# Channel mixing of a two-layer decoder trunk by Strassen's scheme, with weight sums on GpSimd

## What is computed

```python
for l in range(DEPTH):                                   # 2 layers
    u = _rmsnorm(h, norm_mix_pre[l])
    mix, v_first = _mixer(u, ...)
    h = h + _rmsnorm(mix, norm_mix_post[l])
    u = _rmsnorm(h, norm_ffn_pre[l])
    f = jnp.square(jax.nn.relu(u @ w_up[l])) @ w_down[l] # 1024 -> 4096 -> 1024
    h = h + _rmsnorm(f, norm_ffn_post[l])
```

## Time and profile before

| | us |
|---|---|
| median of 3 runs (4385.25 to 4389.9) | 4388.46 |
| the profiled execution | 4390.43 |
| its span, first to last instruction | 4388.7 |

### The profile page before, as it was taken

One profiled execution on the slowest core, in us unless ns is written; L12 is line 12 of the kernel. 1 busy time (PEld: TensorE's weight loads), 2 busy tenths in 40 slices (PEclk: granted clock), 3 DMA queues, 4 the chain that ended last, 5 costly groups with the idle time before them and its releaser, 6 DMA issues.

```text
span 4388.7 us, 66844 instructions
## 1 busy us (share of the span) xinstructions
PE 3986.1 (91%) x28112; PEld 2674.6 (61%) x28112; DVE 1744.9 (40%) x3846; ACT 771.4 (18%) x1536; POOL 213.3 (5%) x188
## 2 busy tenths in 40 slices
PE   7999677999979999999899986869999899999996
PEld 4566455885656666666555654558855566666663
DVE  2599766665140000000247988566641400000002
ACT  1211452331010000000112124523310100000000
POOL 0041000000000000000001310000000000000000
PEclk9999798998989999999999988879979999999997
DMA  2001000001111111111310110100011111111112
GB/s 109 25 29 39 35 18 2 3 3 47 54 58 38 36 36 38 39 33 38 116 34 24 39 29 13 35 2 3 3 62 38 60 37 38 38 34 38 38 38 83
DMA packets 43313, 162.71 MB, mean 37 GB/s; under 512 B 5056, under 2 KB 5072, under 8 KB 42720
## 3 DMA queue, kind: packets, MB, share of 16 engines
q1 hardware_dynamic: 27648, 100.68, 7.6%
q0 software_dynamic: 15456, 58.85, 3.6%
HBM read 135.07 MB, written 23.49 MB: 36 GB/s over the span
## 4 chain that ended last, share of the span: by engine, by line
PE 82%; DVE 13%; issue 3%; ACT 2%; DMA 0%; POOL 0%; DVEq 0%; ACTq 0%; POOLq 0%
PE ps L544 46%; PE ps L576 16%; PE ps L618 7%; PE ps L767 1%; PE ps L779 1%; DVE arena L1207 1%; PE ps L821 1%; PE ps L792 1%; DVE arena L1328 1%; PE ps L588 1%; PE ps L554 1%; DVE arena L1179 1%; DVE arena L1330 1%; DVE arena L1186 1%; DVE arena L1327 1%
## 5 line engine op out<-in xcount | busy, mean ns | idle before, releaser
L544 PE MATMUL ps<-arena,ring 128*128 128x348 f32 x6912 | 2035.4, 458 | 28.8 <-DVE arena L1158 18.9
L544 PEld LDWEIGHTS ps<-arena,ring 128*128 128x128 f32 x6912 | 1321.4, 191 | 743.8 <-issue 42.8
L576 PE MATMUL ps<-arena,ring 128*128 128x348 f32 x2304 | 697.7, 462 | 23.3 <-DVE arena L1158 18.9
L576 PEld LDWEIGHTS ps<-arena,ring 128*128 128x128 f32 x2304 | 437.1, 192 | 282.7 <-issue 54.6
L618 PE MATMUL ps<-arena 64*64 64x64 f32 (+1 forms) x13600 | 513.2, 226 | 97.7 <-DVE arena L1282 43.2
L618 PEld LDWEIGHTS ps<-arena 64*64 64x64 f32 x13600 | 467.9, 135 | 141.9 <-DVE arena L1328 48.8
L1167 DVE TENSOR_TENSOR aux<-arena 128x1044 f32<-128x1044 f32 x32 | 39.9, 1246 | 1068.2 <-ACT arena L938 1068.2
L938 ACT ACTIVATE arena<-ps 128x1044 f32 x96 | 99.9, 1040 | 1971.6 <-PE ps L544 1971.6
L1207 DVE TENSOR_SCALAR_CACHE_REDUCE arena<-arena,little 128x384 uint8<-128x384 f32 (+6 forms) x448 | 416.9, 991 | 3.1
L1561 DVE TENSOR_TENSOR arena<-arena x64 | 79.8, 1246 | 812.2 <-ACT arena L938 812.2
L989 ACT ACTIVATE arena<-ps 128x128 f32<-128x128 f32 x340 | 93.3, 277 | 192.5 <-PE ps L618 192.5
(11 more groups left out here) (202 smaller groups left out, 2612.3 us busy)
## 6 DMA issues: line engine op xcount, KB each, us to landing
ring<-units SPq DMA_DIRECT2D x192, 512.0 KB, 3.6
h_scratch<-arena POOLq DMA_DIRECT2D x24, 522.0 KB, 3.1
arena<-h_scratch POOLq DMA_DIRECT2D x24, 522.0 KB, 7.5
arena<-h_in POOLq DMA_DIRECT2D x16, 522.0 KB, 9.9
out<-arena POOLq DMA_DIRECT2D x8, 522.0 KB, 3.1
arena<-att_scratch POOLq DMA_DIRECT2D x2, 2080.0 KB, 9.0
att_scratch<-arena POOLq DMA_DIRECT2D x16, 256.0 KB, 2.9
aux<-rope POOLq DMA_DIRECT2D x2, 1044.0 KB, 12.4
```

Source lines behind the costliest of these rows:

```text
L544: ins = mm(ps[:, b + s, 0:SW], ring[:, (u % RING) * D + k * P:(u % RING) * D + (k + 1) * P], rhs(g * KT + k)[:, slice_(s)], start=(g == 0 ...
L576: ins = mm(ps[:, b + s, 0:SW], ring[:, r * D + k * P:r * D + (k + 1) * P], tile(U0, k)[:, slice_(s)], start=(k == 0), stop=(k == KT - 1))
```

## The change

Channel mixing is cut into quarters of the 4096 hidden channels. For quarter n, an up step (q = 2n) multiplies a 1024 by 1024 square of `w_up` with the input, and a down step (q = 2n + 1) a square of `w_down` with the 1024 new hidden channels, adding to the output. A step is 4 pairs of units, j = 0 to 3. Units a and b of a pair are cut into halves along their inputs, which gives four blocks of 128 outputs by 512 inputs; the right operand is cut into upper and lower 4 tiles, and left and right SPLIT = 522 tokens. A pair's 2 by 2 product of blocks is formed by Strassen's scheme (Winograd's form) with seven products in place of eight. Each product accumulates over 4 blocks in two slices of HALF = 261 tokens in two banks; four such accumulators take turns.

- The sums of right operands (four a step, 128 by 4 x 522) are VectorE's (`operand_sums`), once for the input and once a quarter for the hidden channels.
- The four sums of weights a pair (128 by 512 each) are GpSimd's (`weight_sums`), in two buffers.
- ScalarE copies out the first product of a pair alone (`first_of`). VectorE adds up all seven (`quarters`), rectifies and squares in one operation (`scalar_tensor_tensor`, max then mult), and in the last step squares the outputs for the norm.
- The SyncE queue is unrolled, follows the new order of units, and refills both slots of a pair when all its seven products are done.
- GpSimd loads `h` again (into `U0`) between the weight sums of q = 6 and q = 7, when q = 6 has ended on TensorE. The load of `small` for layer 1 moves behind the first `h_ready`.
- All of channel mixing is unrolled on TensorE. The output tiles are at `OUT0`; `rstd` and the squares move to `Z0` and behind.

The core of the diff:

```diff
+SPLIT, HALF = W // 2, W // 4
+SQUARES = FFN // D
+PRODUCTS = 7
+PAIRS = 2 * SQUARES * KT // 2
...
+        acc_at = lambda n: ps[:, 2 * (n % 4):2 * (n % 4) + 2, 0:HALF]
...
+            for at in range(DEPTH * UNITS):
+                k = at % RING
+                if at >= RING:
+                    l, pos = divmod(at - RING, UNITS)
+                    if pos < NZ + KT:
+                        sp.wait_ge(S["unit_done"], l * (NZ + KT) + pos + 1)
+                    else:
+                        sp.wait_ge(S["products"], PRODUCTS * (l * PAIRS + (pos - NZ - KT) // 2 + 1))
+                sp.dma_start(ring[:, k * D:(k + 1) * D], units[source(at)]).then_inc(landed[k], 16)
...
+                def weight_sums(l, q, j):
+                    p = l * PAIRS + q * KT // 2 + j
+                    pos, a, b = pair_slots(q, j)
...
+                    for k in (a, b):
+                        pool.wait_ge(landed[k], 16 * ((l * UNITS + pos) // RING + 1))
+                    if p >= 2:
+                        pool.wait_ge(S["products"], PRODUCTS * (p - 1))
+                    for i, x, y, op in ((1, quarter(b, 0), quarter(b, 1), ALU.add),
+                                        (2, w_sum(p, 1), quarter(a, 0), ALU.subtract),
+                                        (3, quarter(a, 0), quarter(b, 0), ALU.subtract),
+                                        (4, quarter(a, 1), w_sum(p, 2), ALU.subtract)):
+                        nc.gpsimd.tensor_tensor(w_sum(p, i), x, y, op).then_inc(S["weights_ready"], 1)
+                        pool.wait_ge(S["weights_ready"], w.next("weights_ready"))
...
-                pool.wait_ge(S["h_stored"], w.next("h_stored", 16 * KT))
-
-                pool.wait_ge(S["unit_done"], (l + 1) * UNITS - (FFN // D - 1))
-                for k in range(KT):
-                    dma(res_at(k), h_dram[k], "h_loaded")
+                for q in range(2 * SQUARES):
+                    for j in range(KT // 2):
+                        weight_sums(l, q, j)
+                    if q == 2 * SQUARES - 2:
+                        pool.wait_ge(S["h_stored"], w.next("h_stored", 16 * KT))
+                        pool.wait_ge(S["products"], PRODUCTS * (l * PAIRS + (2 * SQUARES - 1) * KT // 2))
+                        for k in range(KT):
+                            dma(res_at(k), h_dram[k], "h_loaded")
...
+            def seven(l, q, j):
...
+                fresh = j == 0 and (q == 0 or q % 2 == 1)
+                def product(i, lhs, rhs, sums=0, weights=0, ready=None):
+                    n = PRODUCTS * p + i
+                    if n >= 4:
+                        pe.wait_ge(S["acc_free"], n - 3)
+                    if fresh and sums:
+                        pe.wait_ge(S["sums_ready"], have + sums)
+                    if weights:
+                        pe.wait_ge(S["weights_ready"], 4 * p + weights)
+                    for k in range(KT // 2):
+                        if ready:
+                            pe.wait_ge(S["u_ready"], ready + k)
+                        for s in range(2):
+                            ins = mm(acc_at(n)[:, s], lhs[:, k * P:(k + 1) * P], rhs(k)[:, s * HALF:(s + 1) * HALF],
+                                     start=(k == 0), stop=(k == KT // 2 - 1))
+                    ins.then_inc(S["products"], 1)
...
+                product(0, quarter(a, 0), lambda k: upper(k, 0), sums=1 if q else 0, ready=first)
+                product(1, quarter(a, 1), lambda k: lower(k, 0), sums=3 if q else 0, ready=first and first + 4)
+                product(2, w_sum(p, 2), t_(2), sums=4, weights=2)
+                product(3, w_sum(p, 3), lambda k: upper(k, 1), sums=5, weights=3)
+                product(4, w_sum(p, 1), t_(1), weights=1)
+                product(5, quarter(b, 1), t_(4), sums=6)
+                product(6, w_sum(p, 4), lambda k: lower(k, 1), weights=4)
...
-                project(MT_FFN, lambda k: tile(U0, k), base + NZ + KT, ready=("u_ready", 2 * KT * l + KT, range(1, KT + 1)))
-                pe.wait_ge(S["hid_ready"], w.next("hid_ready"))
-                project(KT, lambda k: tile(HID0, k), base + NZ + KT + MT_FFN, group=FFN // D)
+                for q in range(2 * SQUARES):
+                    for j in range(KT // 2):
+                        seven(l, q, j)
...
+                for p in range(l * PAIRS, (l + 1) * PAIRS):
+                    act.wait_ge(S["products"], PRODUCTS * p + 1)
+                    if p:
+                        act.wait_ge(S["acc_free"], PRODUCTS * (p - 1) + 3)
+                    go(halves(first_of), acc_at(PRODUCTS * p), ACT.Copy).then_inc(S["first_out"], 1)
...
+                fresh = q % 2 == 0 or q == 1
+                if not fresh:
+                    dve.wait_ge(S["first_out"], p + 1)
+                    add(c[0][0], c[0][0], first)
+                dve.wait_ge(S["products"], n + 2)
+                dve.wait_ge(S["first_out"], p + 1)
+                add(c[0][0], first if fresh else c[0][0], m2, 2)
+                if q % 2 == 0:
+                    rectified(c[0][0])
+                dve.wait_ge(S["products"], n + 3)
+                add(c[0][1] if fresh else u, first, m6, 1)
+                if not fresh:
+                    add(c[0][1], c[0][1], u)
+                dve.wait_ge(S["products"], n + 4)
+                add(u, c[0][1] if fresh else u, m7, 1)
+                if not fresh:
+                    add(c[1][1], c[1][1], u)
+                    add(c[1][0], c[1][0], u)
+                dve.wait_ge(S["products"], n + 5)
+                add(c[1][1], u if fresh else c[1][1], m5)
+                add(c[0][1], c[0][1], m5, 1)
+                dve.wait_ge(S["products"], n + 6)
+                add(c[1][0], u if fresh else c[1][0], m4, 1)
...
+                    if k == KT // 2 - 1:
+                        dve.wait_ge(S["u_ready"], w.value("u_ready"))
+                        dve.sem_inc(S["sums_ready"], 1)
+                        operand_sums(U0, TU0, 1, 0, 4)
...
+                        quarters(l, q, j)
+                        if q % 2 == 0 and j == 1:
...
+                            operand_sums(HID0, TH0, 1, 0, 4)
+                        if q % 2 == 0 and j >= 2:
+                            for i in (2, 3, 4):
+                                operand_sums(HID0, TH0, i, 2 * j - 4, 2 * j - 2, last=j == 3)
```

More of the change, by code:

```diff
@@ L421, in _, with source @@
         def _(sp):
[L422 to L429, removed]
+            def source(at):
+                l, pos = divmod(at, UNITS)
+                if pos < NZ + KT:
+                    return at
+                q, i = divmod(pos - NZ - KT, 2 * KT)
+                first = l * UNITS + NZ + KT
+                return first + KT * q + i if i < KT else first + MT_FFN + SQUARES * (i - KT) + q
+            for at in range(DEPTH * UNITS):
+                k = at % RING
+                if at >= RING:
+                    l, pos = divmod(at - RING, UNITS)
+                    if pos < NZ + KT:
+                        sp.wait_ge(S["unit_done"], l * (NZ + KT) + pos + 1)
+                    else:
+                        sp.wait_ge(S["products"], PRODUCTS * (l * PAIRS + (pos - NZ - KT) // 2 + 1))
+                sp.dma_start(ring[:, k * D:(k + 1) * D], units[source(at)]).then_inc(landed[k], 16)
         @block.gpsimd
@@ L601, in out_of @@
                 pe.wait_ge(tri(name), tri_out(l, name))
+            def seven(l, q, j):
+                p = l * PAIRS + q * KT // 2 + j
+                pos, a, b = pair_slots(q, j)
+                raw, t = (U0, TU0) if q % 2 == 0 else (HID0, TH0)
+                have = sums_of(l, 0 if q % 2 == 0 else 1 + q // 2)
+                quarter = lambda k, right: ring[:, k * D + right * 4 * P:k * D + (right + 1) * 4 * P]
+                upper, lower = (lambda k, side: side_of(raw, k, side)), (lambda k, side: side_of(raw, 4 + k, side))
+                t_ = lambda i: (lambda k: t_at(t, i, k, k + 1)[:, 0])
+                fresh = j == 0 and (q == 0 or q % 2 == 1)
[14 more added lines that the diff above has]
+                    ins.then_inc(S["products"], 1)
+                for k in (a, b):
+                    pe.wait_ge(landed[k], 16 * ((l * UNITS + pos) // RING + 1))
+                first = 2 * KT * l + KT + 1 if fresh and q == 0 else None
+                product(0, quarter(a, 0), lambda k: upper(k, 0), sums=1 if q else 0, ready=first)
[5 more added lines that the diff above has]
+                product(6, w_sum(p, 4), lambda k: lower(k, 1), weights=4)
             def pe_chunk(w, odd):
@@ new lines, in quarters, with add, rectified, squared @@
+            def quarters(l, q, j):
+                p = l * PAIRS + q * KT // 2 + j
+                base = HID0 if q % 2 == 0 else OUT0
+                c = [[halves(side_of(base, 2 * j + k, side)) for side in range(2)] for k in range(2)]
+                n = PRODUCTS * p
+                m2, m6, m7, m5, m4, m3 = (acc_at(n + i) for i in range(1, PRODUCTS))
+                first, u = halves(first_of), halves(u_sum)
```

(24 more changed lines are left out.)

89 lines of the change are left out of this document (67 added, 22 removed).

## The result

| | before | after | ratio |
|---|---|---|---|
| median of the first comparison, us | 4389.18 (4 runs) | 4176.20 (4170.34 to 4186.01) | 0.9515, interval 0.9492 to 0.9537 |
| median of a second, 9 runs and 5 | 4391.79 | 4177.89 (4173.12 to 4181.97) | 0.9517, interval 0.9504 to 0.9530 |
| the profiled execution | 4390.43, span 4388.7 | 4186.01, span 4184.1 | |

The change takes 213 us off. 4168 was forecast, from 222.1 us less, with 4150 to 4235 as its range.

The account below looks back on a forecast made before the run. TensorE's streamed matmul columns were taken to bound channel mixing. Its terms, 1577.0 + 12.7 + 1.0 - 0.6 = 1590.1 us in place of 1812.2, took 222.1 off 4390.43, giving 4168; range 4150 to 4235, 8 in 10.

Parts of the forecast that it names:

- What binds: Channel mixing, 1812.2 us for two layers, is bound by TensorE's streamed matmul columns alone; VectorE works 10% there.
- Part 1: Seven products a pair in channel mixing: 7168 records of 261 columns at 220.0 ns, 1577.0 us for both layers.
- the price of a matmul: TensorE's 348-column record costs 292.5 ns, 2.5 fixed; the remaining 1.8 us of half a layer belong to hardware loops.
- Part 2: TensorE's waits for accumulators and sums are met and cost nothing visible, with 7 to 10.6 us of slack.
- rival (a): TensorE's waits between products each expose a 107 ns weight load: +48 us, 4216; 12%.
- Part 3: VectorE's rectification and recombination, at worst 13.1 of 24.64 us a pair, stay hidden, cost 0; both 3.0 us holes go.
- Rival (b): VectorE, held by GpSimd, is late at some products: 1.2 us a pair, +77 us, 4245; 6%.
- Part 4: GpSimd's weight sums in channel mixing take 1.2 us each, 4.9 us a pair, and are ready in time: cost 0.
- The hold between GpSimd and VectorE: Each GpSimd weight sum can hold VectorE for its own length, at most 4.9 us a pair: still hidden, cost zero.
- part 6: GpSimd's reload before the last quarter delays the next weight sums: 0.5 us a layer, 6.6 if sums await the transfers.
- Part 5: At each layer's start the first pair waits for tiles and operand sums: 6.4 us lost, 12.7 for both layers.
- rival (c): Shorter matmuls leave the weight load uncovered: 325 ns a record, 4904 us, slower than before from 251 ns; 4%.

Follow-up runs that it names:

- e1_eight: Changed kernel with the second product of every pair streamed twice, so eight products a pair: 4395.25 us.
- e6_waits: Changed kernel with three more already met waits on the accumulator in each TensorE product from the fifth on: 4170.00 us.
- e5_260: Changed kernel with each matmul streaming 260 columns in place of 261: 4174.30 us.
- e3_pool2: Changed kernel with every GpSimd weight sum computed twice: 4205.24 us.
- e9_order: e8_start with VectorE taking out the first two products between the second and third operand sums: 4165.93 us, ratio 0.9487 to the kernel before.
- e7_reload: Changed kernel with the weight sums of the last quarter's first pair put ahead of the reload of h: 4174.77 us.
- e4_dve2: Changed kernel with each VectorE addition done twice, first into a spare place: 4187.27 us.
- e8_start: e7_reload with each layer's first pair reordered, products without operand sums earlier, VectorE's sums after all tiles: 4175.93 us, ratio 0.9509 to the kernel before.

## Why the prediction held, and where it was off

- **What binds** (first part): right. e1_eight shows it most plainly. VectorE's 10% holds for the up halves alone; in the down halves it is 16.2 of 451 us.
- **Part 1, 220.0 ns a record**: 220.7 measured. 0.7 ns x 7168 = 4.9 us, the largest share of the 7.8 us by which the stage fell less than forecast (214.3 against 222.1). The mechanism was right and the fixed part mis-sized: I took 2.5 ns from 348 columns, and it is 3.2. Neither waits nor the odd count explain the rest (e6_waits, e5_260), and its cause stays open.
- **The 1.8 us put down to hardware loops** (the price of a matmul): this reading was wrong, though nothing in the sum hangs on it. The down half of layer 0 before, from its start and then from 1709.6 us on:

```profile
1705.20:1709.60 4.40, 4.33 (x9) 2.67 (x10) 0.00 (x0) 0.00 (x0) 0.00 (x0) 0.61 0.01 3
1709.60:2156.50 446.90, 446.90 (x1528) 290.42 (x1526) 16.20 (x13) 7.28 (x7) 4.70 (x9) 1.00 0.15 48
```

  In the loops 446.90/1528 = 292.5 ns, as in the unrolled part. What is over lies in the first 4.4 us, at a granted clock of 0.61, behind the 3.0 us hole. The change takes that away with the hole.
- **Part 2, waits**: right at zero, and rival (a) with its 48 us is refuted by e6_waits.
- **Part 3, VectorE hidden**: right. An addition of 522 columns with an operand in PSUM took 699 ns (0.70 forecast), the stage had VectorE at 322.3 of 802.8 us, 40%. Doubling the additions moved the stage by 4.6 us. Rival (b) asked for 77 us; none of it is seen.
- **Part 4, weight sums**: 1.27 us each at their median, 1.2 forecast, and hidden, by e3_pool2 with room for twice as much in the midst of the stage, but not at its start. That the first sums end 0.2 us ahead of the tiles was not in my working; the zero there was right by luck.
- **The hold between GpSimd and VectorE**: it exists as forecast. The prediction has it hidden, and so it is in the midst of the stage; at the reload it lies on the path (part 6). One line of VectorE, its operands told apart (ns min/median/max, first to last start):

```profile
L1336 DVE TENSOR_TENSOR arena<-arena,ps x200: 698/699/701, 1281.9 to 4138.4; 128x522 f32<-128x522 f32 x100
L1336 DVE TENSOR_TENSOR arena<-arena,aux x96: 702/703/1687, 1565.8 to 4129.3; 128x522 f32<-128x522 f32 x96
```

200 additions with one operand in PSUM were never held, and among 96 with both in SBUF some stood up to a microsecond. GpSimd's sums have the same mark, 1261 ns at least and up to 2157. This agrees with the Trainium skill (SBUF — State Buffer, Who interferes with whom): the shared port pair is an exclusive lock, a VectorE instruction with two SBUF inputs contends with a GpSimd instruction that reads SBUF, and one with at most one SBUF input, outside the 2-port modes, does not.

- **Part 5, the start**: third product at +15.15 us after the first tile began, +14.8 forecast: 0.35 a layer. The clock brought no surprise here: it was at 1.00 before the second product began, in both layers. Of the 6.6 us that the first pair loses against seven products of 3.53 (6.4 forecast), e9_order gets 3.8 back.
- **Part 6, the reload**: 1.4 us a layer, 0.5 forecast, 1.9 in all. The step that failed is "the first two sums, 2.4 us": they took 1.29 and 2.17, since the second met VectorE's operand sum (L1320). That is the hold between the two engines, which the prediction had priced at zero. e7_reload removes the hole. The high bound of 6.6, sums behind the transfers, is refuted: the first sum starts as the eighth issue ends.
- **The slower side**, rival (c): 220.7 ns a record, against 251 where it would begin. A load per record is covered as before. (Its 4904 leaves out the 13.1 us of the other terms; with them it is 4917.)
- **The level of the total**: forecast 4168 for the profiled execution, 4186 measured there, 4176 and 4178 as medians. Of the profiled one's 18 us, 8 are the stage's and 10 token mixing's, whose matmuls the change leaves as they were. There, layer 0 began channel mixing 7.0 us later than before, 0.5 of it from before 1042 us. The windows of before and of after over the same gate matmuls, in this order:

```profile
1042.00:1058.00 16.00, 15.21 (x33) 6.78 (x34) 8.08 (x7) 2.08 (x2) 0.00 (x0) 0.78 0.00 0
```

```profile
1042.00:1058.00 16.00, 14.70 (x23) 6.08 (x24) 8.16 (x7) 1.04 (x1) 0.00 (x0) 0.58 0.00 0
```

At a granted clock of 0.78 TensorE did 33 records in those 16 us, at 0.58 it did 23. The clock fell at 1044.6 us in place of 1050.9 and stayed at 0.50 for 54.6 us in place of 40.9. In another execution of the changed kernel channel mixing began at 1245.1, 4.5 us earlier than before, and over the traces of the changed kernel and its variants it began between 1244.8 and 1256.6, with before's 1249.6 in between. The mean granted clock up to there was 0.924 in the first of these and 0.917 in the last. So this part scatters over some 12 us, most of it with the clock, and none of it is shown to come from the change. The other 3 us are token mixing of layer 1, 1279.7 us against 1276.6, where the variants took 1274.7 to 1280.2.

## What to carry to other kernels

When a stage is one unbroken stream of matmuls, fewer columns are paid back nearly one for one (214 us of 910.8 + 909.1, where an eighth would be 227), as long as each record's weight load stays covered and the other engines' work per accumulator fits into the time of the accumulators in flight. What is lost then sits where the stream begins and where a queue mixes two duties, and a hole can cost more than its length, since the clock fell behind three of them (e3_pool2, e4_dve2, e8_start): let the first products be those that need no prepared operand, free their accumulators ahead of later preparations, and put what the next product needs ahead of bulk transfers. Test cover by doubling the covered work; it shows both the reserve and the place that has none.

## What was not expected of the hardware

- 1332 more waits on TensorE, all met, cost nothing that shows: 684.96 us for 3104 records with and without them.
- Holes in TensorE's stream of 2.1, 2.5 and 4.45 us (e8_start, e4_dve2, e3_pool2) went with a granted clock of 0.50 for 3.4, 3.4 and 6.8 us. Not every hole did so: the clock stayed at 1.00 behind the 1.4 us at the changed kernel's reload and behind the 2.25 us in its first pair of layer 0.
- The fixed part of a matmul record is 3.2 ns at 261 columns, 3.0 at 260 and 2.5 at 348.
- GpSimd's additions and VectorE's two-SBUF-input operations alternate when both have a queue of them: four VectorE operations went from 4.96 to 8.85 us, and two GpSimd ones from 2.6 to 4.37.
